# A hybrid decoder step on one core: row numbers gathered per pair of samples, sample outputs turned later, other banks for the ReLU, last rows stored by halves

## The reference

```python
z = rmsnorm(x, g_norm) @ w_in          # 2048 -> 8848 columns, split among all heads
o_r = retention(q_r, k_r, v_r, state)  # 8 heads, chunks of 128 tokens; new states are outputs
score = sum_h w_i[h] * relu(q_i[h] . k_i_all)        # 16 index heads
idx = top_k(score, 128 prompt / 256 sample)
o_a = softmax(q_a . k_g / sqrt(128)) @ v_g           # k_g, v_g: the rows that idx names
x = x + concat(head_norm(o_r) * silu(g_r), o_a * silu(g_a)) @ w_out
y = rmsnorm(x, final_norm_g)
```

## Time and profile before

| | |
|---|---|
| runs | 1211.84, 1218.0, 1218.63 us; median 1218.0 |
| profiled execution | 1213.43 us, span 1211.6 us, mean granted clock 0.990 |
| PE busy | 1173.7 us, 97% of the span |
| DVE, ACT, POOL busy | 627.4, 451.1, 573.9 us (52%, 37%, 47%) |
| three matmul lines L1459 to L1461 | 72% of the span on the chain that ended last |
| HBM | 127.02 MB read, 10.34 MB written |

### The profile page before, as it was taken

One profiled execution on the slowest core, in us unless ns is written; L12 is line 12 of the kernel. 1 busy time (PEld: TensorE's weight loads), 2 busy tenths in 40 slices (PEclk: granted clock), 3 DMA queues, 4 the chain that ended last, 5 costly groups with the idle time before them and its releaser, 6 DMA issues.

```text
span 1211.6 us, 21960 instructions
## 1 busy us (share of the span) xinstructions
PE 1173.7 (97%) x9172; PEld 1110.6 (92%) x9172; DVE 627.4 (52%) x1199; ACT 451.1 (37%) x791; POOL 573.9 (47%) x262
## 2 busy tenths in 40 slices
PE   7999999999999999999999989999999999999995
PEld 5999996557999999999999989999999998999994
DVE  6600005999997975999997234433352544010013
ACT  5322225774223332434423324243425353232332
POOL 2355555241343333333536576855666384545450
PEclk9999999999999999999999989999999999999998
DMA  7333436380333222223332425545453426432213
GB/s 245 105 113 106 137 106 245 125 288 2 105 105 105 70 71 72 70 75 90 99 108 70 107 70 142 133 126 138 109 150 85 141 71 211 129 99 86 87 35 141
DMA packets 152840, 138.58 MB, mean 114 GB/s; under 512 B 4653, under 2 KB 145053, under 8 KB 151069
## 3 DMA queue, kind: packets, MB, share of 16 engines
q1 hardware_dynamic: 144502, 110.72, 30.6%
q0 software_dynamic: 6976, 22.03, 5.4%
q10 hardware_dynamic: 1280, 4.66, 1.1%
HBM read 127.02 MB, written 10.34 MB: 113 GB/s over the span
## 4 chain that ended last, share of the span: by engine, by line
PE 89%; DVE 6%; POOL 1%; issue 1%; ACT 1%; DMA 1%; another core or an unknown queue 0%; DVEq 0%; ACTq 0%; POOLq 0%
PE bank L1459 24%; PE bank L1460 24%; PE bank L1461 24%; PE bank L1477 6%; PE bank L1690 1%; PE bank L1672 1%; PE bank L1572 1%; PE bank L1602 1%; DVE bm L1094 1%; DVE XT L1027 1%; POOL rowf L903 1%; DMA XT<-in_x_prompt 1%; PE bank L1611 1%; PE bank L1714 1%; PE bank L1847 0%
## 5 line engine op out<-in xcount | busy, mean ns | idle before, releaser
L1459 PE MATMUL bank<-Hh,Wh 128*128 128x264 f32 (+2 forms) x2432 | 712.5, 293 | 3.0 <-POOL Wl L851 2.8
L1460 PE MATMUL bank<-Hl,Wh 128*128 128x264 f32 (+2 forms) x2432 | 704.3, 290 | 0.4 <-issue 0.4
L1461 PE MATMUL bank<-Hh,Wl 128*128 128x264 f32 (+2 forms) x2432 | 702.9, 289 | 0.7 <-issue 0.7
L851 POOL TENSOR_TENSOR Wl<-Wraw,Wh 128x2048 fp32r<-128x2048 f32 x84 | 386.6, 4603 | 468.0 <-ACT Wh L490 467.6
L1459 PEld LDWEIGHTS bank<-Hh,Wh 128*128 128x128 f32 x2432 | 460.6, 189 | 7.9 <-issue 4.2
L1460 PEld LDWEIGHTS bank<-Hl,Wh 128*128 128x128 f32 x2432 | 460.4, 189 | 3.3 <-issue 2.9
L1461 PEld LDWEIGHTS bank<-Hh,Wl 128*128 128x128 f32 x2432 | 459.5, 189 | 0.9 <-issue 0.9
L490 ACT ACTIVATE Wh<-Wraw 128x2048 fp32r<-128x2048 f32 x84 | 160.4, 1911 | 362.0 <-PE bank L1461 361.8
L1398 DVE TENSOR_TENSOR Y<-Y,bank 128x512 f32 (+1 forms) x16 | 10.4, 684 | 163.5 <-PE bank L1477 163.5
L1077 DVE COPY QS<-mix 128x128 f32<-128x128 f32 x1 | 0.3, 277 | 140.5 <-ACT mix L496 140.5
L879 POOL DMA_INDIRECT kx<-in_cache_kidx,pidx x32 | 30.3, 947 | 40.6 <-PE bank L1477 34.9
(11 more groups left out here) (258 smaller groups left out, 1249.8 us busy)
## 6 DMA issues: line engine op xcount, KB each, us to landing
Wraw<-in_w_in SPq DMA_DIRECT2D x36, 1024.0 KB
Wraw<-in_w_in SPq DMA_DIRECT2D x64, 512.0 KB
Wraw<-in_w_out SPq DMA_DIRECT2D x16, 1024.0 KB
XT<-in_x_prompt ACTq DMA_DIRECT2D x4, 1024.0 KB, 9.3
sp__98<-in_state_ret SPq DMA_DIRECT2D x8, 512.0 KB, 4.0
out<-sp__98 SPq DMA_DIRECT2D x8, 512.0 KB, 5.2
Y<-in_x_prompt SPq DMA_DIRECT2D x1, 4096.0 KB
out<-Y SPq DMA_DIRECT2D x4, 1024.0 KB
```

Source lines behind the costliest of these rows:

```text
L851: nc.gpsimd.tensor_tensor(Wl[:, a, :, :], Wraw[:, a, :, :], Wh[:, a, :, :].bitcast(F32), ALU.subtract).then_inc(w_lo, 1)
L1459: mm(bank[i][:, 0:w], wh, Hh[:, kk, s], start=(a == 0 and k == 0), stop=False)
L1460: mm(bank[i][:, 0:w], wh, Hl[:, kk, s], start=False, stop=False)
L1461: last = mm(bank[i][:, 0:w], wl, Hh[:, kk, s], start=False, stop=(a == 1 and k == KC - 1))
```

## The change

- POOL no longer gathers 16 columns of `rowf` in head 2 around `rotary`; it gathers four columns (two halves for each of two samples) behind both `rotary` calls of heads 2, 3, 4 and 5, each time for the pair of the next head. DVE makes `isnew` and `rowu` for these four columns at the end of each of these heads, and POOL's wait for `row_ready` counts with the head.
- The ReLU of the index scores writes banks 0 and 1; the turned head weights go to bank 2. The fourth key turn waits for `wsel`; the first two row products wait for the last accumulation.
- The turn of `OSn` moves from ahead of the second chunk of block 35 to behind its first part.
- `rsqrt` makes its guess in one instruction instead of two (13 calls).
- The sum of squares of the first seven output blocks is formed ahead of the last one; the last is added in one instruction.
- ACT's scaling of blocks 0 and 2 and DVE's of block 3 are cut at column 1024; blocks 2 and 3 are stored by column halves, the left half of 3 first. Six stores of `Y` instead of four.

```diff
...
@@ -455,12 +456,14 @@
-            for i, by_act, by_dve in ((0, 1, 1), (1, 1, 3), (2, 2, 4), (3, 2, 6)):
+            left, right, whole = slice(0, DM // 2), slice(DM // 2, DM), slice(0, DM)
+            for i, c, by_act, by_dve in ((0, whole, 2, 1), (1, whole, 2, 3), (3, left, 2, 4), (2, left, 3, 4), (2, right, 4, 5),
+                                         (3, right, 4, 7)):
                 sp.wait_ge(fin_act, by_act)
                 sp.wait_ge(fin_dve, by_dve)
-                store(y_prompt[0, P * i:P * i + P, :], Y[:, i, :])
-            sp.wait_ge(fin_dve, 7)
-            sp.wait_ge(fin_act, 3)
+                store(y_prompt[0, P * i:P * i + P, c], Y[:, i, c])
+            sp.wait_ge(fin_dve, 8)
+            sp.wait_ge(fin_act, 5)
             store(y_sample.rearrange("b o m -> (b o) m"), Ys[:, :])
@@ -633,13 +636,13 @@
                         act.wait_ge(acc_free, 36)
-                    nc.scalar.activation(bank[1 + i % 2][:, 0:w], bank[4 + i % 4][:, 0:w], ACT.Relu).then_inc(si_relu, 1)
+                    nc.scalar.activation(bank[i % 2][:, 0:w], bank[4 + i % 4][:, 0:w], ACT.Relu).then_inc(si_relu, 1)
                     i += 1
...
             nc.scalar.activation(wsel[:, :, :].rearrange("p g (s x) -> p g s x", s=SEC)[:, :, :, 0:NS],
-                                 bank[0][:, 0:2 * NS].rearrange("p (g b) -> p g b", g=2).unsqueeze(2).to_broadcast([P, 2, SEC, NS]),
+                                 bank[2][:, 0:2 * NS].rearrange("p (g b) -> p g b", g=2).unsqueeze(2).to_broadcast([P, 2, SEC, NS]),
                                  ACT.Copy).then_inc(wsel_ready, 1)
@@ -815,7 +818,8 @@
                 act.wait_ge(y_gain, 7)
-                nc.scalar.activation(Y[:, i, 0:LASTC], Y[:, i, 0:LASTC], ACT.Copy, scale=st4[:, 40 + i:41 + i]).then_inc(fin_act, 1)
+                for c in (slice(0, DM // 2), slice(DM // 2, LASTC)):
+                    nc.scalar.activation(Y[:, i, c], Y[:, i, c], ACT.Copy, scale=st4[:, 40 + i:41 + i]).then_inc(fin_act, 1)
@@ -897,9 +901,9 @@
-            def candidate_rows(which):
-
-                for m in which:
+            def candidate_rows(j):
+
+                for m in (2 * j, 2 * j + 1, NS + 2 * j, NS + 2 * j + 1):
                     nc.gpsimd.indirect_dma_start(rowf[:, m:m + 1], None, row_table, bass.IndirectOffsetOnAxis(
@@ -931,7 +935,7 @@
                 if 0 < h - HP <= 4:
-                    pool.wait_ge(row_ready, 1)
+                    pool.wait_ge(row_ready, h - HP)
                     pool.wait_ge(sk_tr, 2 * (h - HP - 1))
@@ -939,17 +943,14 @@
                 lo(n + 1, 0)
+                rotary(h, 0)
+                lo(n + 1, 1)
+                rotary(h, 1)
                 if h == HP:
...
                     pool.wait_ge(posu_ready, 1)
-                    candidate_rows(range(NS))
-                rotary(h, 0)
-                if h == HP:
-                    candidate_rows(range(NS, NS + 2))
-                lo(n + 1, 1)
-                rotary(h, 1)
-                if h == HP:
-                    candidate_rows(range(NS + 2, 2 * NS))
+                if 0 <= h - HP < 4:
+                    candidate_rows(h - HP)
                 if 0 < h - HP <= 4:
@@ -999,8 +1000,7 @@
                 y, z = rsq[0:r, 0, 0:w], rsq[0:r, 1, 0:w]
-                link(v_.tensor_scalar(y.bitcast(I32), x.bitcast(I32), 1, None, ALU.arith_shift_right))
-                link(v_.tensor_scalar(y.bitcast(I32), y.bitcast(I32), -1.0, float(0x5f3759df), ALU.mult, ALU.add))
+                link(v_.tensor_scalar(y.bitcast(I32), x.bitcast(I32), -0.5, float(0x5f3759df), ALU.mult, ALU.add))
                 for step in range(3):
...
@@ -1356,10 +1356,12 @@
                 topk(8 if h != HP - 1 else 6 * SELS)
-                if h == HP:
-                    dve.wait_ge(rowf_in, 16 * 2 * NS)
-                    v_.tensor_scalar(isnew[:, :], rowf[:, :], NEWROW / 2, None, ALU.is_gt)
-                    v_.tensor_scalar(rowu[:, :], rowf[:, :], float(cache_k.shape[1] * P - 1), None, ALU.min).then_inc(row_ready, 1)
+                if 0 <= h - HP < 4:
+                    dve.wait_ge(rowf_in, 64 * (h - HP + 1))
+                    pair = [x[:, :].rearrange("p (f b) -> p f b", f=2)[:, :, 2 * (h - HP):2 * (h - HP) + 2]
+                            for x in (rowf, isnew, rowu)]
+                    v_.tensor_scalar(pair[1], pair[0], NEWROW / 2, None, ALU.is_gt)
+                    v_.tensor_scalar(pair[2], pair[0], float(cache_k.shape[1] * P - 1), None, ALU.min).then_inc(row_ready, 1)
                 if 0 < h - HP <= 4:
@@ -1403,8 +1405,8 @@
                 s = st4[:, 40 + a:40 + b]
-                link(v_.tensor_reduce(s, ysq[:, a:b, :], AXX, ALU.add))
-                link(v_.tensor_scalar(s, s, 1.0 / DM, EPS, ALU.mult, ALU.add))
+                v_.scalar_tensor_tensor(s, ysq[:, a:b, 7], 1.0 / DM, ysum[:, a:b], ALU.mult, ALU.add).then_inc(y_mean, 1)
+                dve.wait_ge(y_mean, 2 if a else 1)
                 rsqrt(s, y_rs)
@@ -1412,11 +1414,16 @@
-            def other_blocks(i):
-                v_.tensor_scalar(Y[:, i, 0:LASTC], Y[:, i, 0:LASTC], st4[:, 40 + i:41 + i], None, ALU.mult).then_inc(fin_dve, 1)
+            def other_blocks(i, c):
+                v_.tensor_scalar(Y[:, i, c], Y[:, i, c], st4[:, 40 + i:41 + i], None, ALU.mult).then_inc(fin_dve, 1)
+
+            left, right = slice(0, DM // 2), slice(DM // 2, LASTC)
...
                 y_block(Step(dve, k, (256, 0), (3, 1), (3, 2), (3, 3)))
+            dve.wait_ge(y_sq, 35)
+            link(v_.tensor_reduce(ysum[:, :], ysq[:, :, 0:7], AXX, ALU.add))
+            link(v_.tensor_scalar(ysum[:, :], ysum[:, :], 1.0 / DM, EPS, ALU.mult, ALU.add))
             y_block(Known(7), (0,))
@@ -1424,14 +1431,15 @@
             dve.wait_ge(y_gain, 7)
-            other_blocks(1)
+            other_blocks(1, slice(0, LASTC))
             y_block(Known(7), (1, 2))
...
             dve.wait_ge(y_rs, 2)
+            other_blocks(3, left)
             last_block(2)
             last_block(3)
-            other_blocks(3)
+            other_blocks(3, right)
             v_.scalar_tensor_tensor(Ys[:, LASTC:DM], Ys[:, LASTC:DM], st4[0:NS, 44:45], gfb[0:NS, LASTC:DM], ALU.mult, ALU.mult)
@@ -1573,7 +1581,7 @@
             for g in range(2):
-                last = turn(bank[0][:, NS * g:NS * g + NS], wsT[:, g, :, :].rearrange("a b h -> a (b h)"), NS)
+                last = turn(bank[2][:, NS * g:NS * g + NS], wsT[:, g, :, :].rearrange("a b h -> a (b h)"), NS)
             last.then_inc(ws_tr, 1)
@@ -1585,7 +1593,7 @@
                 elif u == 3:
-                    pe.wait_ge(si_acc, i)
+                    pe.wait_ge(wsel_ready, 1)
                 elif u:
@@ -1607,7 +1615,8 @@
                 pe.wait_ge(sc_relu, G + 1)
-                pe.wait_ge(wsel_ready, 1)
+                if G < 2:
+                    pe.wait_ge(si_acc, i)
                 mm(bank[half][32 * half:32 * half + NS * SEC, :], wsel[:, g, NS * SEC * s:NS * SEC * s + NS * SEC],
@@ -1868,9 +1877,12 @@
             chunk(NB_IN, 0, {1: lambda: outputs(NH - 1), 3: lambda: turn_outputs(NH - 1)})
-            pe.wait_ge(gs_n, 1)
-            turn(bank[7][:, 0:P], OSn[:, :]).then_inc(gs_tr, 1)
-            chunk(NB_IN, 1)
+            def turn_samples():
+
+                pe.wait_ge(gs_n, 1)
+                turn(bank[7][:, 0:P], OSn[:, :]).then_inc(gs_tr, 1)
+
+            chunk(NB_IN, 1, {1: turn_samples})
             chunk(NB_IN + 1, 0)
```

More of the change, by code:

```diff
@@ L114, in build @@
         ysq = sb("ysq", [P, 5, 8])
+        ysum = sb("ysum", [P, 5])
         bnst = sb("bnst", [P, 4, 6])
@@ L260, in build @@
         pads_zero = sem("pads_zero"); kp_done = sem("k_pad_done"); vp_done = sem("v_pad_done"); qz_done = sem("q_windows_done"); vs_ev = sem("vs_ev"); m_hi = sem("m_hi"); ms_hi = sem("m_samples_hi"); ms_lo = sem("m_samples_lo"); m_lo = sem("m_lo_even"); m_lo2 = sem("m_lo_odd")
-        y_res = sem("y_res"); y_tr = sem("y_tr"); y_add = sem("y_add"); y_sq = sem("y_sq"); y_gain = sem("y_gain"); y_rs = sem("y_rs")
+        y_res = sem("y_res"); y_tr = sem("y_tr"); y_add = sem("y_add"); y_sq = sem("y_sq"); y_gain = sem("y_gain"); y_rs = sem("y_rs"); y_mean = sem("y_mean")
         fin_act = sem("fin_act"); fin_dve = sem("fin_dve")
@@ L1090, in _ @@
                     dve.wait_ge(si_relu, i + 1)
-                    relu = bank[1 + i % 2][:, 0:w]
+                    relu = bank[i % 2][:, 0:w]
                     if h:
```

## The result

The changed kernel takes 1236.6 us in the median of four runs (1235.76 to 1237.78), the kernel before took 1215.8 beside it (1211.84 to 1218.63): a ratio of 1.0164, with an interval of 1.0136 to 1.0192. It is slower by 1.6%, against a forecast of 1206. The profiled execution took 1235.85 us with a span of 1233.5, 21.9 us more than before.

A forecast was written before the change was run, and what follows sets the result against it. PE was taken to bound the kernel (89% of the chain), with gains only in its waits, halved clock and both ends. 0.4 + 0.9 + 5.8 + 2.4 + 1.6 = 11.1 us gave 1206.9 from the median 1218.0, stated as 1206, range 1197 to 1214.

The forecast's parts named there:

- Start and ReLU banks: Shorter rsqrt in DVE's chain at the start wins 0.4 us; no wait on bm at the fourth key turn, 0.9.
- Head 2: With the gathers behind rotary and Wl, head 2 wins all 10.1 us it loses to waits and halved clock.
- the 2.2 us without a listed cause: Part of head 2's 10.1 us that no listed wait explains; counted to the gathers and expected to go.
- Row numbers, first point: Head 3: later Wl makes vst, then vx, late for L1851; 0.7 us lost.
- Row numbers, second point: Heads 3 to 6: PE waits 0.9 us each for the kg copies, 3.6 us lost, bounds 0 and 6.
- (c): Pauses at the turn of kg reach 2 us and halve the clock in four heads: 1222 us, chance 0.05.
- (a): Longer row-number chain in heads 3 to 6, 1.5 us more in each of four heads: 1212 us, chance 0.2.
- Sample outputs: Turning OSn one part later replaces 2.0 us wait and 1.7 clock loss by 1.3 us wait: 2.4 us won.
- the end: Shorter rsqrt, split scaling and half-column stores from about 1203.0 win 1.6 us at the end, range 0.6 to 2.0.
- Rival (d): The store halves don't help and the end wins nothing: 1208 us, chance 0.05.

The follow-up runs named there:

- E2: Kernel before with only the row-number part of the change: 1239.0 us, 1.0188 of the kernel before.
- E12: E6 with the old banks again (ReLU in banks 1 and 2, the weights' turn in bank 0): 1201.0 us.
- E6: E4 with each head's four row-number gathers moved ahead of the second rotary step, apart from the vg gathers: 1201.2 us, 0.9887 of the kernel before.
- E3: Changed kernel, but POOL's second weight subtraction in heads 3 to 6 waits for the finished kg copies: 1211.0 us, 0.995 of the kernel before.
- E4: Changed kernel, but DVE makes the pair's numbers mid-head behind kst, not at the head's end: 1208.4 us, 0.9932 of the kernel before.
- E1: Changed kernel with the row numbers as in the kernel before, all 16 gathers in head 2: 1210.5 us, 0.9957 of the kernel before.
- E10: E6 with the turn of the sample outputs (OSn) put back where it was before: 1202.2 us.
- E11: E6 with the last rows scaled and stored whole again, the shorter square root kept: 1200.1 us.
- E9: Changed kernel with POOL's second weight subtraction of heads 3 to 6 in two half-size instructions, nothing between them: 1229.3 us.
- E8: E4 with the turn of the sample outputs put back where it was before: 1212.9 us.

## Why the prediction was wrong

**Start and ReLU banks (0.4 + 0.9).** Not settled. The first mark came 2.7 us sooner, but over the eleven kernels that have both parts it lies anywhere from 620.99 to 624.88; E2, which has neither, has 623.21, and E12, with the old banks, 622.94. The wait on bm goes, as forecast; a gain is not shown.

**Head 2 (10.1).** Right: 52.39 us from mark to mark, 10.1 less, the 2.2 us without a listed cause among them. E6 has the same 52.39.

**Row numbers, first point (vst and vx of head 3).** Not seen in the changed kernel, and of no weight. With the later pace Wl ended at 772.27 and vst took 0.39 us. At the pace that the prediction assumed the point holds: in head 3 of E6 vst takes 2.87 us, and PE waits 0.5 us on vx, where 0.7 was forecast.

**Row numbers, second point: the step that failed.** It says: "But there PE had lost 1.4 to 1.7 us to the halved clock. Without it PE comes at 737.2 to 737.5 and waits 0.8 to 1.1 us for the copies. I take 0.9, in four heads: 3.6 us." I moved PE ahead by what the clock had cost, and left everything else in place. But ACT's Wh waits for PE, and POOL's second Wl for Wh: it moves ahead with PE, into the last copy. In the trace of before 0.65 us of room kept the two apart, less than the 1.4 to 1.7 by which I let PE come sooner. What stood there instead of 0.9 us was 5.0 of waiting and 2.3 of clock, some 29 in four heads (E3 and E4 won back 25.6 and 28.2). E1 shows it with the old row numbers.

The rule was at hand. SBUF — State Buffer of the Trainium skill, section "SBUF: two separate sides", has an exclusive lock between DVE operations with two inputs in SBUF and GpSimd operations that read SBUF, held for a whole instruction by the one that starts first; I cited from it only what it says of descriptors. The runs agree, with 4.73 us under a subtraction of 4.6 and 2.58 under one half as long; the copy of 5.52 us in E6, which began ahead of the subtraction and was held too, is not explained by who starts first. My own first point used the same effect: vst, 2.54 us under a Wl. I applied it to one DVE operation and not to the copies 15 us later.

**Rivals.** (c) named the place and the sign, pause plus clock in four heads, with 1222 and a chance of 0.05. Its cause, a chain 1.1 us longer, was not the one that came, and its 4.7 us per head was 7.3. (a), the longer chain, is refuted as the main cause: the four gathers into kg take 4.75 to 4.78 us in heads 3 to 6 of the changed kernel, 4.73 in head 3 of the trace of before, and E3 leaves the chain 0.7 us per head, less than the 0.9 that the sum had for it.

**What was not on the list.** The gaps at the end of eight gathers in a row, with the halved clock behind them in head 3 (769.9 to 773.3), 2.5 us in each of heads 3 to 5, some 7 us. I had the 2.2 us without a cause in head 2 of before, counted them to the gathers, and did not carry them to heads 3 to 5, where the change puts four gathers ahead of the four into vg. Half of the 2.2 us can be read in the trace of before: PE's gaps in head 2, at the end of the eight gathers from 684.83 to 694.56.

```profile
694.78 0.38 PE L1460 MATMUL bank<-Hl,Wh 128*128 128x264 f32 x1 [0.44 <-issue]
...
696.21 0.38 PE L1461 MATMUL bank<-Hh,Wl 128*128 128x264 f32 x1 [0.69 <-issue]
```

How the gathers hold up PE is open: these gaps have no releaser in the records.

**Sample outputs (2.4) and the end (1.6).** Together 4.0 forecast, 3.4 measured behind the last mark. The turn: PE waits 1.5 us on Hl instead of 2.0 on OSn, at full clock, where the third of the halved windows of the earlier trace rows stood; E10 gives 1.9 for one profile, 1.0 in the medians. The end: from the last matmul to the end 13.1 us instead of 14.4, so 1.25 won: 0.8 by the store halves (E11) and 0.4 by the square root, as forecast. The halves fell short because the last 2 MB take 0.3 us longer, not the 0.1 to 0.2 that I had put on them without a row for it, and the hole shrank by 1.05 us and not by 1.7. Rival (d), halves that win nothing, is refuted by the profiles; the medians alone can't tell it.

## What to carry to other kernels

When a stall is removed, move every engine that was paced by it, not only the one that stood: list what else waits on the faster engine, and see which of its instructions now land on top of each other. A short DVE copy out of SBUF beside a long GpSimd operation takes its own length or what is left of the other, and tenths of a microsecond decide which; a wait that puts the long operation behind the short ones (0.7 us later on POOL in E3) can be a cheap cure. And a chain measured in one disturbed head is to be rebuilt, instruction by instruction, for the undisturbed pace.

## What the runs showed of the hardware

- A predicated DVE copy of 128 x 256 words takes 0.43 us alone and waits for the end of a GpSimd subtraction that it meets, and ends 0.3 us behind it: up to 4.73 us with one of 4.6 us, 2.58 with one of half the size. Between two subtractions that follow each other at once it gets in (E9). Between a gather and a subtraction it did not: begun 0.6 us ahead of the subtraction, it took 5.5 us (E6, three heads).
- A small DVE operation with one input waits too: isnew, 128 x 4, took 3.28 us under a Wl in E4, where 0.16 is its length in the changed kernel.
- At the end of eight indirect DMAs in a row on POOL, 1.25 us apart, PE has gaps of 0.4 to 0.8 us, 1.4 to 1.7 us per head in E4, whose heads 3 to 5 are 1.3 to 4.0 us longer than those of E6; two groups of four with 4.3 us of other work between them leave none (E6).
- A pause of PE of 0.7 us left the clock at 1.00 (E3); behind one of 2.0 us it fell in the profile of E10 and stayed at 1.00 in that of E8. Of the four pauses of 2.8 us in E9, the clock fell to 0.50 behind the first and the last and stayed at 1.00 behind the other two.
